# Narrow experts of a mixture-of-experts layer: unsplit 32-bit weights in two 64-column groups, and a ring of ten slots

## What is computed

```python
def swiglu(x, wg, wu, wd):
    return (jax.nn.silu(x @ wg) * (x @ wu)) @ wd

def moe_swiglu(x, w_router, b_router, wg, wu, wd):
    logits = (x @ w_router).astype(jnp.float32) + b_router.astype(jnp.float32)
    top_v, top_i = lax.top_k(logits, TOP_K)
    top_w = jax.nn.softmax(top_v, axis=-1)
    combine = jnp.sum(jax.nn.one_hot(top_i, N_EXPERTS, dtype=jnp.float32) * top_w[..., None], axis=-2)
    combine = combine.astype(x.dtype)
    out = jnp.zeros_like(x)
    for e in range(N_EXPERTS):
        out = out + combine[..., e:e + 1] * swiglu(x, wg[e], wu[e], wd[e])
    return out
```

## Time and profile before

| what | value |
|---|---|
| three runs | 1319.69, 1319.85, 1325.71 us |
| profiled execution, first to last instruction | 1319.5 us |
| TensorE busy | 1267.1 us (96%), 6161 matmul records |
| VectorE busy | 1129.3 us (86%) |
| ScalarE busy | 929.9 us (70%) |
| moved by DMA | 425.10 MB, mean 322 GB/s |

### The profile page before, as it was taken

How to read it: one execution, slowest core, us unless ns; L and a number is a source line. 1 busy time by engine, 2 the same in 40 slices (tenths; PEclk the granted TensorE clock), 3 DMA queues, 4 the chain that set the end, 5 groups by cost and what they waited for, 6 DMA issues and landing times.

```text
span 1319.5 us, 16344 instructions
## 1 busy us (share of the span) xinstructions
PE 1267.1 (96%) x6161; PEld 1033.9 (78%) x6161; DVE 1129.3 (86%) x944; ACT 929.9 (70%) x747; POOL 92.8 (7%) x111
## 2 busy tenths in 40 slices
PE   7989999999999999999999999999999999999996
PEld 6987888888977778778877777887777787677774
DVE  5887644457988899999998999898999989899997
ACT  5555444435544788888886888887888888788883
POOL 2660000000750000000000000000000000000000
PEclk9999999999999999999999999999999999999998
DMA  9637555544352999999999999999999999999992
GB/s 310 234 127 242 186 189 190 192 160 160 130 172 83 396 394 375 389 399 404 409 409 409 389 411 394 409 409 409 399 388 405 398 409 409 409 390 402 397 406 93
DMA packets 133045, 425.10 MB, mean 322 GB/s; under 512 B 9008, under 2 KB 11344, under 8 KB 132960
## 3 DMA queue, kind: packets, MB, share of 16 engines
q1 hardware_dynamic: 131600, 420.21, 83.7%
q0 software_dynamic: 1216, 3.71, 0.9%
q10 hardware_dynamic: 144, 0.07, 0.0%
HBM read 422.91 MB, written 1.05 MB: 321 GB/s over the span
## 4 chain that ended last, share of the span: by engine, by line
PE 70%; DVE 16%; issue 7%; ACT 4%; SPq 1%; DMA 1%; DVEq 0%; ACTq 0%
PE bank L1783 18%; PE bank L1785 17%; PE bank L1784 17%; DVE w_lo L1182 8%; PE bank L2117 6%; PE bank L2118 5%; DVE arena L1285 1%; DVE w_lo L1204 1%; PE bank L2163 1%; DMA raw<-in_w_in 1%; PE bank L2150 1%; ACT w_hi L841 1%; DVE parts L1655 1%; PE bank L2091 1%; PE bank L2113 1%
## 5 line engine op out<-in xcount | busy, mean ns | idle before, releaser
L1182 DVE TENSOR_TENSOR w_lo<-raw,w_hi 128x2048 fp32r<-128x2048 f32 x216 | 485.9, 2286 | 31.6 <-PE bank L1785 16.0
L821 ACT CAST w_hi<-raw 128x2048 fp32r<-128x2048 f32 x216 | 408.0, 1916 | 62.7 <-PE bank L1785 61.4
L1783 PE MATMUL bank<-w_hi,parts 128*128 128x512 f32 x824 | 328.6, 399 | 13.1 <-DVE w_lo L1182 7.3
L1785 PE MATMUL bank<-w_hi,parts 128*128 128x512 f32 x824 | 321.5, 390 | 0.0
L1784 PE MATMUL bank<-w_lo,parts 128*128 128x512 f32 x824 | 321.0, 390 | 0.0
L2117 PE MATMUL bank<-w_hi,parts 128*128 128x512 f32 x672 | 270.9, 403 | 8.4 <-ACT arena L1048 3.0
L2118 PE MATMUL bank<-w_lo,parts 128*128 128x512 f32 x672 | 263.6, 392 | 0.0
L1783 PEld LDWEIGHTS bank<-w_hi,parts 128*128 128x128 f32 x824 | 154.8, 188 | 55.4 <-issue 21.2
L1204 DVE TENSOR_TENSOR w_lo<-raw,w_hi 128x2048 fp32r<-128x2048 f32 x60 | 138.6, 2311 | 60.8 <-PE bank L1785 46.3
L1182 DVE TENSOR_TENSOR w_lo<-arena,w_hi 128x2048 fp32r<-128x2048 f32 x80 | 181.1, 2286 | 2.3 <-ACT w_hi L821 2.0
L1785 PEld LDWEIGHTS bank<-w_hi,parts 128*128 128x128 f32 x824 | 154.7, 188 | 33.0
(11 more groups left out here) (260 smaller groups left out, 1262.3 us busy)
## 6 DMA issues: line engine op xcount, KB each, us to landing
raw<-in_wu_exp SPq DMA_DIRECT2D x76, 1024.0 KB, 11.3
raw<-in_wg_exp SPq DMA_DIRECT2D x70, 1024.0 KB, 10.3
raw<-in_wd_exp SPq DMA_DIRECT2D x70, 1024.0 KB, 10.7
arena<-in_wd_exp SPq DMA_DIRECT2D x29, 1024.0 KB, 10.4
arena<-in_wg_exp SPq DMA_DIRECT2D x26, 1024.0 KB, 11.0
arena<-in_wu_exp SPq DMA_DIRECT2D x25, 1024.0 KB, 10.7
raw<-in_w_in SPq DMA_DIRECT2D x20, 1024.0 KB, 5.8
tokens<-in_wg_exp SPq DMA_DIRECT2D x16, 1024.0 KB, 11.9
```

What stands on the lines that cost most here:

```text
L821: a.copy(to, ring[s]).then_inc(hi_ready, 1)
L1182: v.tensor_tensor(low(n), ring[s], high(n).bitcast(F32), ALU.subtract).then_inc(lo_ready, 1)
L1783: mm(psum, left[0], right[0], start=first, stop=False)
L1785: return mm(psum, left[1], right[0], start=False, stop=last)
```

## The change

Narrow units are no longer rounded nor subtracted. TensorE multiplies the 32-bit numbers in the ring slot directly, with 64 stationary columns, and each unit's columns are halved: the left half goes to PSUM partitions 0 to 63 and the right half to partitions 64 to 127 of one bank, one matmul each, in turn. So the gate and the up product of a block of 1024 take one bank each (`GATE_B` 6, `UP_B` 7) with 128 rows, their activation and product have 128 x 512 elements instead of 64 x 1024, and the fold with its shift matrix is gone. The hidden values are turned by 128 x 128 transposes, half as many, and kept in 32 bits. The gathered narrow tokens are summed from their high and low parts by VectorE (`take_narrow`).

A ring slot with a narrow unit is free when TensorE has multiplied it (`unit_done`), one with a wide unit as before (`slot_free`). The ring has ten slots, of which `raw` gives seven; `SLOT` goes over ten of them three times in a pair and then over nine. Buffers of `w_hi` and `w_lo` go to wide units alone, so "three ahead" now skips narrow units.

```diff
-RAW = 6
+RAW = 7
...
-RING = 9
-SLOT = [s for n in (9, 9, 9, 9, 8, 8, 8, 8, 8, 8) for s in range(n)]
+RING = 10
+SLOT = [s for n in (10, 10, 10, 9, 9, 9, 9, 9, 9) for s in range(n)]
...
+            def slot_free(p, v):
+
+                if is_wide(p, v):
+                    sp.wait_ge(lo_ready, split_count(p, v))
+                else:
+                    sp.wait_ge(unit_done, done(p, v))
...
-                        sp.wait_ge(lo_ready, done(p, before[-1]))
+                        slot_free(p, before[-1])
...
-                round_unit(SLOT[v], high(v), landing(p, v), done(p, v - HIGH))
+                if is_wide(p, v):
+                    o = wide_before(p, v)
+                    round_unit(SLOT[v], high(o), landing(p, v), wide_done(o - HIGH))
...
-                subtract_unit(SLOT[n], n, done(p, n), done(p, n - SPLIT))
+                if is_wide(p, n):
+                    o = wide_before(p, n)
+                    subtract_unit(SLOT[n], o, split_count(p, n), wide_done(o - SPLIT))
...
+            def take_narrow(p, q):
+                dve.wait_ge(xg_ready, gathered(p, q)[1])
+                ks = slice(2 * q, 2 * q + 2)
+                lo = bank[GATHER_BANKS[1]][:, 0:2 * BOTH].rearrange("p (k c) -> p k c", c=BOTH)[:, :, P:]
+                v.tensor_tensor(xg_n[:, ks, :], xg_n[:, ks, :], lo, ALU.add).then_inc(xgn_ready, 1)
...
-            def one_pass(psum, left, right, first, last):
-                mm(psum, left, right[0], start=first, stop=False)
-                return mm(psum, left, right[1], start=False, stop=last)
...
+            def unit_narrow(p, v, kind, b, q):
+
+                pe.wait_ge(*landing(p, v))
+                width = D if kind == "d" else EXP_WIDTH[b]
+                n, kn, half = {"d": SUM_B, "g": GATE_B, "u": UP_B}[kind], UNIT // width, width // 2
+                w = ring[SLOT[v]].rearrange("p (k n) -> p k n", n=width)
+                for kk in range(kn):
+                    k = kn * q + kk
+                    left = eh_n[:, k, :] if kind == "d" else xg_n[:, k, :]
+                    first = k == 0 and (kind != "d" or b == 0)
+                    final = b == EXP_BLOCKS - 1 and k == EXP_WIDTH[b] // P - 1 if kind == "d" else k == DK - 1
+                    for h in range(2):
+                        last = mm(bank[n][h * NARROW:(h + 1) * NARROW, 0:half], left,
+                                  w[:, kk, h * half:(h + 1) * half], start=first, stop=final)
                 last.then_inc(unit_done, 1)
...
             def turn_b(i, b):
                 pe.wait_ge(eh_ready, 2 * EXP_BLOCKS * i + (2 * b + 2))
-                pe.sem_inc(turn_go, 1)
-                for j in range(EXP_WIDTH[b] // P):
-                    last = tr(bank[WORK_B][:, j * NARROW:(j + 1) * NARROW], esg_n[0:NARROW, j * P:(j + 1) * P],
-                              ident[0:NARROW, 0:NARROW])
+                for c in range(EXP_WIDTH[b] // (2 * P)):
+                    last = tr(bank[GATE_B][:, c * P:(c + 1) * P], esg_n[:, c * P:(c + 1) * P], ident)
                 last.then_inc(eturn_b, 1)
-
-            def add_lower(b, c0):
-                for hf in range(EXP_WIDTH[b] // HALF):
-                    last = mm(bank[WORK_B + hf], shift, fold[:, c0 + hf * HALF:c0 + (hf + 1) * HALF],
-                              start=False, stop=True, skip_group_check=True)
-                last.then_inc(fold_mm, 1)
```

More of the change, by code:

```diff
@@ L325, in build @@
         pick, pick_n = pick_both[:, :, 0:P], pick_both[:, :, P:]
[L326 to L330, removed]
         esg = carve([EBLK], 2048)
-        esg_n = carve([EBLK])
+        esg_n = carve([HALF])
+        xg_n, eh_n = (carve([DK, NARROW]) for n in range(2))
         y_a = carve([D])
@@ L1039, in take_extra, with take_b, gate_silu @@
                 a.copy(four(xg_hi, n), bank[GATHER_BANKS[0]]).then_inc(xg_ready, 1)
-            def take_b(banks):
-                for n in range(2):
-                    act.wait_ge(gather_b, n + 1)
-                    a.copy(four(xg_n, n), bank[banks[n]]).then_inc(xgn_ready, 1)
-            def gate_silu(b, to, n, rows):
-                w = EXP_WIDTH[b]
-                a.activation(to[0:rows, 0:w], wide_bank(n, w, rows), ACT.Silu).then_inc(esilu, 1)
+            def take_b():
+                act.wait_ge(gather_b, 1)
+                a.copy(xg_n.rearrange("p k c -> p (k c)"), bank[FIRST_B_BANK]).then_inc(xgn_first, 1)
+            def gate_silu(to, psum):
+                a.activation(to, psum, ACT.Silu).then_inc(esilu, 1)
             def hidden_high(i, b):
@@ L2129, in unit @@
                             j = 2 * q + jj
-                            left = (eh_hi[:, j, :], eh_lo[:, j, :]) if stream == "A" else eh_n[:, j, :]
                             r = (slice(None), jj, slice(hw * HALF, (hw + 1) * HALF))
-                            last = times(bank[sums + hw], left, (w[0][r], w[1][r]), b == 0 and q == 0 and jj == 0,
-                                         b == EXP_BLOCKS - 1 and q == 1 and jj == 1)
+                            last = product(bank[SUM_A + hw], (eh_hi[:, j, :], eh_lo[:, j, :]), (w[0][r], w[1][r]),
+                                           b == 0 and q == 0 and jj == 0, b == EXP_BLOCKS - 1 and q == 1 and jj == 1)
                 else:
                     width = EXP_WIDTH[b]
-                    w = halves(v, width)
+                    w = halves(o, width)
                     kn = UNIT // width
@@ L2187, in start_block @@
                     elif (stream, kind) == ("B", "u"):
[L2188 removed]
+                        if b or not first:
+                            pe.wait_ge(eh_ready, 2 * EXP_BLOCKS * p + 2 * b)
                     elif stream == "A" and not late:
```

269 lines of the change are left out of this document (126 added, 143 removed).

## The result

Four runs of the changed kernel gave a median of 1308.98 us (1308.13 to 1309.42), and the kernel before, on the same chip, 1321.51 us: a ratio of 0.990 with a 95% interval of 0.988 to 0.992. The forecast was 1310. The profiled execution's span fell from 1319.5 to 1306.4 us. Wherever both were recorded for one execution, its time is 1.7 to 2.0 us above its span (1308.13 and 1306.4 us here); so the span of 1319.5 us belongs to an execution of some 1321 us (an estimate from that difference), and a run's time isn't the few tenths above it that were taken before the change.

The account below looks back on a forecast made before the run. The DMA floor of expert weight loads, 216.1 us a pair, was taken to hold once waits went: 1319.5 - 8 (expert stretch) - 2 (behind the last byte) = 1309.5 us of span, plus 0.35, so 1310 us; range 1302 to 1356.

Parts of the forecast that it names:

- DMA floor: Expert weight loads of a pair: 76 units at 410 GB/s and 8 at 386, together 216.1 us, against 219.2 taken.
- The four holes: Four stretches, one in each pair, where the DMA rate fell to 362 to 375 GB/s; forecast to go.
- Half of 16 us in the stretch: Expert loads from 428 to 1291 us: at most 16 us to gain by reaching full DMA rates; 8 us taken.
- Side by side: Narrow units on TensorE: the two column halves run at once, 1.72 us a unit instead of 3.44 one after the other.
- rival 1: Narrow units' weight loads don't hide behind the other half's passes: 1341 us at 0.08 us a load; chance 0.20.
- rival 2: Narrow units' two halves don't overlap at all on TensorE: 57.7 us more a pair, 1551 us; chance 0.12.
- TensorE's work in a pair stays at 211.0 us: TensorE in a pair of experts: 82.7 us of narrow work added against 82.6 removed.
- What they are worth is what waited for them: Narrow subtractions (96 us a pair, VectorE) and roundings (80, ScalarE) removed: worth only the 8 us a pair of waits.
- I cost this at nothing: Narrow slots held until multiplied: nine to ten slots hold 23 us of loading, against a 6.9 us scatter lump; cost nothing.
- Rival 3: Halves overlap, but slots held longer take back VectorE's relief and holes in the DMA rate stay: 1319 us; chance 0.15.
- It gives no earlier start: The tenth ring slot lies behind eight wide units loadable before the narrow expert is known, so loading starts no earlier.
- The lag behind the last byte: From the last byte to the last scatter: 9 us now, 5.7 at best; 2 of these 3.6 us taken as gain.

Follow-up runs that it names:

- half_loads: The changed kernel with only the first half of every narrow unit loaded, all matmuls, roundings and subtractions kept: 1273.1 us, ratio 0.964.
- one_group: The changed kernel with both column halves of a narrow matmul sent through the same 64-column group of the array: 1556.46 us.
- nine_slots: The changed kernel with the ring of before, nine slots, six of them from the earlier phases: 1311.32 us, ratio 0.992.
- halves_apart: The changed kernel with a narrow unit's two loops exchanged, all matmuls of the left half, then all of the right: 1307.62 us in one run.

## Why the prediction was right

- **The bound.** A DMA floor of 216.1 us a pair: right in kind, and 1.4 us low. The changed kernel takes 217.5 us a pair from load to load, and the loads hold it (half_loads). The four holes are closed, as forecast, and VectorE is busy for 337.15 of 657 us. One sign that was asked for did not come: the scatter was to stand 216 to 217 us after the last, and in the last three pairs it stands 218.95 and 217.66 us apart.

```profile
686.85 1.88 PE L2125 MATMUL bank<-arena 128*128 128x512 f32 x4
...
905.80 1.88 PE L2125 MATMUL bank<-arena 128*128 128x512 f32 x4
...
1123.46 1.88 PE L2125 MATMUL bank<-arena 128*128 128x512 f32 x4
```

  Nor does TensorE wait for landings by name. Its waits from 538 to 1195 us are still put down to `w_lo`, now of a unit that has just landed, as in the chain above:

```profile
PE bank L1791 <- DVE w_lo L1193: 26.4, 22, 2.7
```

- **Half of 16 us in the stretch.** By the windows from 428 us the 8 us taken came as 3.0 in the first pair and 4.9 in the next three, 7.9, but that holds part of the earlier start. From the first narrow landing to the last it is 5.1 us. The expectation that the floor would not be reached was right, but for another reason. It was not the scatter or late first units: it was the new hole of 4.1 us, and the pairs' 217.5 us against 216.1.
- **Side by side.** Right: 1.755 us a unit with entry and exit, against 1.72 and 0.08 for each change. The rule of the Trainium skill (page "TensorE: Matmul & The Clock Gate", section "Part 3: Packing small matmuls") that stood beside rival 1 would have every load of 64 columns uncovered, since all use the full rows. The trace disagrees: 32 loads of 0.14 us lie inside a group of 7.02 us. The Trainium skill's sentence beside rival 2 (page "TensorEngine Tiling (Array Packing)", section "Key Properties"), that tiles load and multiply in parallel, agrees with the traces, and one_group shows what it is worth: 13.95 against 7.02 us.
- **"TensorE's work in a pair stays at 211.0 us": wrong**, by 4.4 us against 206.6. Three terms were mis-sized. The passes without a partner, 4.7 us and another 1.7 around the narrow transposes, don't exist, since passes don't start in the order of the program. And the scatter was taken to cost what it did, 6.9 us; its narrow part now uses 64 rows in each of two halves, and those run side by side as well, two scatters in the changed kernel's chain being

```profile
1123.62 1.72 PE bank L2125 x4
1125.34 1.06 PE bank L2130 x4
1129.34 1.72 PE bank L2125 x4
1131.06 1.06 PE bank L2130 x4
```

  5.6 us for the same 16 passes. 211.0 - 4.7 - 1.7 - 1.3 is 203.3. The third term goes the other way: entering and leaving the 64-column form was taken at 0.08 each, 0.16 together. The first pass of the group above starts 0.32 us after the matmul ahead of it, where 0.227 is a step, so 0.09 late; 0.14 are lost inside the group; and behind a group the second matmul is 0.34 us after the first, 0.11 late:

```profile
740.28 0.50 PE L1791 MATMUL bank<-w_hi,parts 128*128 128x512 f32 x1
740.62 0.40 PE L1792 MATMUL bank<-w_lo,parts 128*128 128x512 f32 x1
```

  That is 0.34 in place of 0.16. For twelve groups and four transposes inside them, it would be 2.9 of the 3.3 us between 203.3 and 206.6, an estimate from these places; the rest isn't placed.
- **"What they are worth is what waited for them": half the story.** VectorE's relief would do alone in the middle pairs, but so would the rest of the change, in which TensorE's shorter work was put at nothing (82.7 us against 82.6). The pairs came out near the forecast because the loads cap the sum of the two.
- **"I cost this at nothing"** (slots held longer): right for the scatter, where SyncE waits up to 7.9 us for the narrow line in one piece (680 to 700 us) and the rate stays at 407 to 411 GB/s from 685 to 720 us; wrong in the first pair, 4.1 us. Rival 3's mechanism is real in that one place: TensorE multiplies eight wide units and gathers before the narrow slots come free, and ten slots don't cover it.
- **"It gives no earlier start"** (the tenth slot): wrong, 3.1 us by the windows to 428 us and 5.1 by the first narrow landing, and nine_slots is 2.3 us slower. The slot is one of `raw`, which the phases before the experts use as well and into which wide units are loaded before the narrow expert is known. So the first narrow unit no longer has to wait for the slot `tokens`.
- **The lag behind the last byte:** 2 us taken of 3.6, 3.1 measured (6.1 us, where 5.7 was called the best).
- **The time above the span:** 0.35 us taken, 1.7 measured.

So the mechanism was right in the main, side-by-side passes and waits that go until the loads hold, but the nearness of 1310 to 1308.98 is in part luck. The sum's 1309.85 us, with 2.9 us less from the stretch, 5.1 of earlier start, 1.1 more from the lag, 0.2 of longer tail and 1.4 more above the span, is 1309.85 + 2.9 - 5.1 - 1.1 + 0.2 + 1.4 = 1308.15 us, and the profiled execution took 1308.13: errors of up to 5 us cancel.

## What to carry to other kernels

Where three resources stand within a few per cent of each other, the gain of a change is the distance to the next of them, not the work removed: taking 96 us of VectorE's work out of a pair, with all else, bought 1.7 in the middle pairs. Before a relief is credited with a gain, give it alone, and then give back what it removed in the changed kernel; here the two tests pointed different ways, because what else the change holds did the same. And where buffers are freed by a later consumer, look at the longest run of held units at the start, where no steady state covers it.

## What the runs showed of the hardware

- 32-bit matmuls of 64 columns in two column groups run at once: two passes of 512 columns for each 0.43 us, with both weight loads of the next step (0.14 us for 64 columns) hidden. In one group the same passes take 0.43 us each.
- The order within the unit didn't matter here: four passes of one half ahead of the other half's four (halves_apart, 7.07 us a group) are paired all the same.
- Matmuls of 64 rows in the two row halves overlap too: 1.06 us for four passes of 512 columns in the scatter, where two at a time would be 0.86 and one by one 1.72.
